# Eight long matmuls, then eight short ones: the order inside a half unit of the first feed-forward product

## What is computed

```
h = rms_norm(x, norm_ffn_g[l])
x = x + jnp.square(jax.nn.relu(h @ w_ff1[l])) @ w_ff2[l]
```

## Time and profile before

| | |
|---|---|
| three runs | 2797.34, 2799.57, 2800.74 us |
| the profiled execution, its own time | 2800.51 us |
| span from its first to its last instruction | 2798.8 us |
| PE busy | 2781.9 us, 99% of the span, 15872 matmuls |
| weight loads (PEld) busy | 2424.8 us, 87% |
| DVE, ACT busy | 1930.7 us (69%), 1351.7 us (48%) |
| granted TensorE clock | 0.999 of full speed |

### The profile page before, as it was taken

The page is one execution under the profiler, slowest core; times in us unless marked ns, Lnnn a source line. Parts: engine busy times, 40 slices in busy tenths (PEclk is TensorE's granted clock), DMA queues, the critical chain, the costliest instruction groups (busy, mean ns, idle before and its releaser), DMA issues.

```text
span 2798.8 us, 38749 instructions
## 1 busy us (share of the span) xinstructions
PE 2781.9 (99%) x15872; PEld 2424.8 (87%) x15872; DVE 1930.7 (69%) x2513; ACT 1351.7 (48%) x1726; POOL 59.3 (2%) x102
## 2 busy tenths in 40 slices
PE   9999999999999999999999999999999999999998
PEld 8899888888888888888888888888888888888887
DVE  7645567778766658898988885556667656666656
ACT  5434654447444436555555543544345434444434
POOL 0000210000000000000000000000000000000000
PEclk9999999999999999999999999999999999999999
DMA  7454444565545544334344455554354455554553
GB/s 273 182 191 158 145 173 187 196 235 191 208 173 203 184 173 170 147 143 151 135 148 148 156 176 196 197 190 164 141 208 183 183 208 189 202 206 185 191 200 151
DMA packets 72849, 506.66 MB, mean 181 GB/s; under 512 B 8384, under 2 KB 8512, under 8 KB 12896
## 3 DMA queue, kind: packets, MB, share of 16 engines
q1 hardware_dynamic: 71136, 497.83, 48.3%
q0 software_dynamic: 1104, 5.90, 0.6%
q10 hardware_dynamic: 432, 0.45, 0.0%
HBM read 499.95 MB, written 2.10 MB: 179 GB/s over the span
## 4 chain that ended last, share of the span: by engine, by line
PE 96%; DVE 2%; ACT 1%; DMA 1%; issue 0%; SPq 0%; POOL 0%; DVEq 0%; ACTq 0%
PE double L1389 89%; PE bank L1389 7%; PE bank L1392 1%; DVE wlo L2101 0%; DMA vec<-in_vec 0%; DMA raw<-in_wall 0%; ACT whi L1759 0%; DVE cacc L2107 0%; DVE acc L2101 0%; SPq L2904 0%; DVE AA L2107 0%; DMA mblk<-in_memT 0%; DVE cst L2124 0%; DVE nacc__124 L2101 0%; DVE nacc__125 L2101 0%
## 5 line engine op out<-in xcount | busy, mean ns | idle before, releaser
L1389 PE MATMUL double<-AA,whi 128*128 128x512 f32 (+1 forms) x5008 | 1619.4, 376 | 3.9 <-DVE wlo L2101 3.8
L1759 ACT ACTIVATE whi<-raw 128x1024 fp32r<-128x1024 f32 x926 | 924.9, 1048 | 797.4 <-PE double L1389 764.8
L1389 PE MATMUL double<-AA,wlo 128*128 128x256 f32 (+1 forms) x4624 | 1280.7, 277 | 0.0
L2101 DVE TENSOR_TENSOR wlo<-raw,whi 128x1024 fp32r<-128x1024 f32 (+1 forms) x934 | 1100.1, 1213 | 193.8 <-ACT whi L1759 190.8
L1389 PEld LDWEIGHTS double<-AA,whi 128*128 128x128 f32 x5008 | 916.1, 188 | 175.6 <-DVE wlo L2101 5.5
L1389 PEld LDWEIGHTS double<-AA,wlo 128*128 128x128 f32 x4624 | 866.1, 187 | 1.3
L1389 PE MATMUL double<-whi,AA 128*128 128x512 f32 x1536 | 481.3, 388 | 0.0
L1389 PEld LDWEIGHTS double<-whi,AA 128*128 128x128 f32 x1536 | 288.4, 188 | 54.0 <-DVE wlo L2101 0.2
L1389 PE MATMUL double<-whi,BB 128*128 128x512 f32 x1024 | 309.5, 382 | 0.0
L1389 PE MATMUL double<-wlo,AA 128*128 128x512 f32 x768 | 295.3, 385 | 0.0
L1389 PEld LDWEIGHTS double<-whi,BB 128*128 128x128 f32 x1024 | 191.8, 187 | 33.8
(11 more groups left out here) (338 smaller groups left out, 1721.0 us busy)
## 6 DMA issues: line engine op xcount, KB each, us to landing
raw<-in_wall SPq DMA_DIRECT2D x462, 1024.0 KB, 4.8
raw<-in_wall SPq DMA_DIRECT2D x9, 256.0 KB, 6.8
X<-in_xT SPq DMA_DIRECT2D x1, 2048.0 KB, 11.2
Mm<-in_memT POOLq DMA_DIRECT2D x1, 2048.0 KB, 16.1
tmp<-rqk POOLq DMA_DIRECT2D x16, 128.0 KB, 2.2
mblk<-in_memT SPq DMA_DIRECT2D x8, 256.0 KB, 4.2
dec<-in_dec POOLq DMA_DIRECT2D x1, 1536.0 KB, 9.2
hs<-in_hsT SPq DMA_DIRECT2D x4, 272.0 KB, 5.6
```

Source lines behind the costliest of these rows:

```text
L1389: return q.matmul(out, lhsT, rhs, start=start, stop=stop, skip_group_check=True)
L1759: q.activation(hi_of(j)[:, c], raw[j % RAW][:, c], ACT.Copy).then_inc(S("w_hi"), 1)
L2101: return q.tensor_tensor(out, a, b, o)
```

## The change

For the units of `f1` alone the body of the loop is replaced. In each half unit all long matmuls are written first (4 k-tiles x 2 groups = 8), and behind them all short ones (8). Which numbers are multiplied, the access patterns, the wait at the head of the half, the wait for the activations of each k-tile, the bank and the count-up at the unit's end stay as they are.

```diff
+        def longs(j, half, i, both, wh, out, first, last):
+            for m in range(2):
+                mm_group(leap(out[:, m * 512:(m + 1) * 512], 4, 8), wh[:, i, m * 128:(m + 1) * 128], leap(flat(both), 4, 8), start=first, stop=False)
+
+        def shorts(j, half, pr, wl, out, last):
+            pi, k, kt, nc_ = units[j]
+            step = 8 if leads(j) else 4
+            for i in range(half * kt // 2, (half + 1) * kt // 2):
+                hh = operand(pr, k * kt + i)[:, 0, :]
+                for m in range(2):
+                    ins = mm_group(leap(out[:, m * 512:m * 512 + T], step, 4), wl[:, i, m * 128:(m + 1) * 128], leap(hh, step, 4),
+                                   start=False, stop=last and i == (half + 1) * kt // 2 - 1)
+            return ins
...
+                if pr["tag"] == "f1" and not split:
+                    longs(j, half, i, both, wh, out, first, last)
+                    if i == (half + 1) * kt // 2 - 1:
+                        ins = shorts(j, half, pr, wl, out, last)
+                    continue
```

## The result

The changed kernel takes 2805.29 us, the median of seven runs (2804.50 to 2810.43); the kernel before took 2798.55 us in the seven runs beside it. The ratio is 1.0029, with a 95% interval of 1.0020 to 1.0039: slower, by 6.7 us in the medians (which alone give 1.0024, inside the interval). The text ahead forecast no change (2800 us) and gave a slowing by over 0.2% a chance of 0.25.

The account below looks back on a forecast made before the run. The prediction took PE, never waiting, to be bound by distances between matmul starts. Long ones at 226 ns and short ones at 114 summed to 0 us change, hence 2800 us; the range ran from 2792 less half a us to 2808.

Parts of the forecast that it names:

- What bounds the kernel: Feed-forward part: PE is busy 99% of the span and never waits from 2139.84 us on, so distances between matmul starts set time.
- What does not move: Around f1: waits, ACT, DVE and SP's loads see the same events, f2 blocks stay at 42.30 us, the clock stays full.
- The long ones in a row: f1's runs of eight long matmuls: bounds 220 and 230 ns each from f2, 226 taken, as in the alternation before.
- The short ones in a row: f1's runs of eight short matmuls: bounds 112 and 116 ns each, possibly 123; 114 taken, as before.
- The sum: Each f1 half: 8 x 226 + 8 x 114 = 2.72 us as before, 0 us change; edges 8 to 9 gained, 12 lost.
- Why the middle: f1 pairs: each matmul still runs beside one load, whose length hardly matters, so swapping loads was priced at nothing.
- The slower one: Rival: every f1 run of long matmuls opens like f2 at 230 ns, shorts 116 to 123; 8 us lost, 2808 us, chance 0.27.
- The faster one: Rival: f1 runs settle at once, long 220 ns, short 112 to 114; 7 to 9 us less, 2792 us, chance 0.22.
- Loads that no longer hide: Rival: each short f1 matmul pays its load's 187 ns instead of 114; 75 us lost, 2875 us, chance 0.02.
- Own time and median: Whole kernel: profiled execution 2800.51 us, median of three runs 0.9 below its span; with 0 change, the median rounded up, 2800 us.

## Why the prediction was right or wrong

**What bounds the kernel: right.** PE has no wait from 2140 us on in any of the runs but those without short matmuls, and every difference there is one of distances between starts.

**What does not move: right.** No wait appeared, `f2` stayed at 42.28 us, and the clock at full.

**The long ones in a row: both bounds occur, the choice between them was wrong.** The 220 of the settled `f2` is what the first half of a block has, the 230 of its opening is what nearly all others have, or a little more (231.9 on average). The value taken, 226, is in neither; it stood for the alternation's pace. The step that failed is "I take 226, between them": the rows show two states, and a mean of two states was priced, weighted by nothing but its place. That a run need not settle stood in the trace of the kernel before, in matmuls of kind N with 512 columns which the prediction did not read (the stretch, then PE and the weight loads of the matmuls that read `AA`):

```profile
885.90:913.40 27.50, 27.49 (x119) 22.50 (x120) 0.00 (x0) 0.00 (x0) 1.00 0.55 196
```

That is 229 to 231 ns each for a run of some 120, while the `f2` blocks of the same trace, once settled, keep 220 to their end.

**The short ones in a row: too low.** 118.6 on average against 114, above the scaled row of the first product (116) and below its unscaled 123. The lower bound of 112 was no row for them: the kernel writes four plain float32 matmuls of 128 columns for each head there, and the trace has eight steps of 112 ns for them, two to a matmul.

**The sum.** 0 us was forecast, 9.3 us is what the stretch costs in the traces: 6 ns x 1024 for the long ones and 4 x 1024 for the short ones, 10 us for eight blocks like those of the later rounds. One edge in the prediction is off by a little: 44 ns a half are reached at 230 with 116 (346 ns a pair against 341), not with 117.

**Why the middle.** That the length of a load weighs little was right for the long ones: with 32 columns loaded they keep 228 ns. It was not for the short ones, 118.6 to 113.3 on average. But nothing about the pace followed from it: the pace hangs on a state that is handed on from matmul to matmul, and the change of order changes what is handed on.

**The rivals.** The slower one came true, at 2805.3 where it had 2808, and in the place that it named, the long run behind a short one. Its mechanism was half right. The runs do open badly, but not because eight matmuls are too few to settle: sixteen and 88 do not settle either. The faster one appeared as far as it could, in the half behind `f2`, and with another first pattern in nearly all halves. Loads that no longer hide did not occur: short matmuls in a row, each with its own load, stand 118.6 ns apart on average. The rule of the Trainium skill that the prediction sets beside this rival stands on the named page, "TensorE: Matmul & The Clock Gate", in the section "The mechanism" and not in the one named.

**Own time and median.** The median moved by 6.7 us and not by 9.3, most likely because executions differ between 700 and 1050 us too (4.8 us in the two traces); that part was not foreseen, and its frequency stays open. It was also luck for the forecast: the median lies inside the range, which ends at 2808 us for the slower rival's sake, but the three runs at 2809.3 to 2810.4 lie above it.

## What to carry to other kernels

Where the matrix engine never waits, a change of order is not free: read the distance between starts of runs of equal matmuls, look at whether a trace shows one pace or more for the same instruction, and where it shows more, give each a chance of its own and ask what the run will be entered with. The first matmul of a run is worth trying in another pattern, and it has to be measured: here it was worth 1.5 us a block in runs of eight and cost 0.5 us a block in the alternation. And compare stretch by stretch: with a state that comes and goes elsewhere, two whole executions differed by 4.0 us where the changed stretch differed by 9.3.

## What the runs showed of the hardware

- Matmuls of type fp32r with 512 columns and a 128 x 128 load each ran in a row at 219 to 221 ns or in a repeating pattern of 227 to 237 (230 on average), at the full clock in both, for as long as nothing else came between: long ones for 52 and for 55, `f2` blocks for nearly all of their 192, with the same tiles and instructions. Other slow patterns held too, 228 and 232 in turn for sixteen and 232 to 235 for 192.
- Code that is not changed takes over the state: `f2` blocks of 192 matmuls took 42.3 or 44.3 to 44.8 us, by what ran ahead of them.
- Once, behind a stop of PE of some 0.2 us, the fast cycle changed to the slow one. From the second round on no stop in the two runs without short matmuls led to the fast one.
- What the cycles are physically is open. The length of the load (32 or 128 columns) and the jumps of the stream each shift the paces, and neither is the cause alone.
